# The prologue of a pooling and sparse-attention decoder step: keys' rows loaded ahead of the input, running means taken behind the pooling product, pooling groups in falling width

## The reference, cut to what matters

```
def _pool_mix(ext, pos0):              # ext: 15 earlier normed rows, then the new ones
    c = cumsum(ext, axis=1)
    for g, w in enumerate((2, 4, 8, 16)):
        s = c[..., 16:16+S, sl] - c[..., 16-w:16-w+S, sl]
        cnt = minimum(w, pos + 1)
        outs.append(s / cnt - xf[:, 15:, sl])

hn = _rmsnorm(h, norms_l[0])
ext = concatenate([buf, hn], axis=1)
mix = einsum('bsgc,gcd->bsgd', _pool_mix(ext, pos0), w_pool_l).reshape(B, S, D_MODEL) * scale_l
h = h + _rmsnorm(mix, norms_l[1])
```

## Time and profile before

| | |
|---|---|
| median of 3 runs | 2551.07 us (2548.14 to 2552.21) |
| profiled execution | 2551.54 us, of which the traced span is 2550.0 us |
| PE, PE weight loads | 2499.5 us (98%), 2462.4 us (97%) |
| DVE, ACT, POOL | 1195.7 us (47%), 924.1 us (36%), 268.3 us (11%) |
| DMA | 400.66 MB, mean 157 GB/s |
| first product that the result needs, pooling product, feed-forward group | start at 15.06, 50.21 and 114.01 us |

### The profile page before, as it was taken

How to read it: one execution, slowest core, us unless ns; L and a number is a source line. 1 busy time by engine, 2 the same in 40 slices (tenths; PEclk the granted TensorE clock), 3 DMA queues, 4 the chain that set the end, 5 groups by cost and what they waited for, 6 DMA issues and landing times.

```text
span 2550.0 us, 44217 instructions
## 1 busy us (share of the span) xinstructions
PE 2499.5 (98%) x17440; PEld 2462.4 (97%) x17440; DVE 1195.7 (47%) x1354; ACT 924.1 (36%) x1157; POOL 268.3 (11%) x316
## 2 busy tenths in 40 slices
PE   7999999999999999999999999999999999999997
PEld 7899999999999999999997799999999999999997
DVE  7564444444444444643535733744444444444444
ACT  5554233323332333632325633633233233323332
POOL 0420000000000001300002311400000000000012
PEclk9999999999999999999999999999999999999999
DMA  6444444444444444455445464344444444444443
GB/s 248 167 143 150 150 164 148 143 154 164 148 156 156 148 149 153 144 161 177 159 167 194 166 187 161 116 148 153 159 148 148 153 159 149 151 160 153 150 149 131
DMA packets 89738, 400.66 MB, mean 157 GB/s; under 512 B 13788, under 2 KB 24940, under 8 KB 60114
## 3 DMA queue, kind: packets, MB, share of 16 engines
q1 hardware_dynamic: 78066, 377.82, 43.7%
q0 software_dynamic: 6160, 12.60, 1.5%
q10 hardware_dynamic: 5456, 9.52, 1.1%
HBM read 392.16 MB, written 19.02 MB: 161 GB/s over the span
## 4 chain that ended last, share of the span: by engine, by line
PE 89%; DVE 5%; ACT 3%; issue 1%; POOL 1%; DMA 1%; SPq 0%; ACTq 0%; DVEq 0%
PE ps L1455 28%; PE ps L1456 28%; PE ps L1457 28%; PE ps L1556 2%; ACT w_hi L524 1%; DVE w_lo L863 1%; ACT y L631 0%; ACT x_hi L549 0%; DMA rowsK<-cmp_data_dram 0%; PE ps L1582 0%; POOL sc L1420 0%; DVE x_lo L881 0%; ACT sq L557 0%; DVE ps L905 0%; DMA rowsV<-cmp_data_dram 0%
## 5 line engine op out<-in xcount | busy, mean ns | idle before, releaser
L1455 PE MATMUL ps<-x_hi,w_hi 128*128 128x320 f32 x3536 | 1095.0, 310 | 6.7 <-DVE sg L1084 2.5
L1457 PE MATMUL ps<-x_hi,w_lo 128*128 128x320 f32 x3536 | 1093.1, 309 | 0.0
L1456 PE MATMUL ps<-x_lo,w_hi 128*128 128x320 f32 x3536 | 1093.1, 309 | 0.0
L863 DVE TENSOR_TENSOR w_lo<-w_raw,w_hi 128x2048 fp32r<-128x2048 f32 (+1 forms) x362 | 744.4, 2056 | 646.7 <-ACT w_hi L524 646.7
L524 ACT CAST w_hi<-w_raw 128x2048 fp32r<-128x2048 f32 (+1 forms) x362 | 619.0, 1710 | 506.1 <-PE ps L1457 479.6
L1455 PEld LDWEIGHTS ps<-x_hi,w_hi 128*128 128x128 f32 x3536 | 664.2, 188 | 9.1 <-DVE sg L1084 3.0
L1456 PEld LDWEIGHTS ps<-x_lo,w_hi 128*128 128x128 f32 x3536 | 664.2, 188 | 0.4 <-issue 0.2
L1457 PEld LDWEIGHTS ps<-x_hi,w_lo 128*128 128x128 f32 x3536 | 664.1, 188 | 0.0
L1457 PE MATMUL ps<-hid_hi,w_lo 128*128 128x320 f32 x1408 | 435.1, 309 | 0.0
L1455 PE MATMUL ps<-hid_hi,w_hi 128*128 128x320 f32 x1408 | 435.1, 309 | 0.0
L1456 PE MATMUL ps<-hid_lo,w_hi 128*128 128x320 f32 x1408 | 435.1, 309 | 0.0
(11 more groups left out here) (266 smaller groups left out, 1459.7 us busy)
## 6 DMA issues: line engine op xcount, KB each, us to landing
w_raw<-w_in_dram SPq DMA_DIRECT2D x176, 1024.0 KB, 4.9
w_raw<-w_out_dram SPq DMA_DIRECT2D x128, 704.0 KB, 4.1
w_raw<-w_kv_dram SPq DMA_DIRECT2D x24, 1024.0 KB, 6.8
w_raw<-w_q_dram SPq DMA_DIRECT2D x17, 1024.0 KB, 4.9
w_raw<-w_o_dram SPq DMA_DIRECT2D x15, 1024.0 KB, 5.2
win_out_dram<-win_kv_dram POOLq DMA_DIRECT2D x8, 992.0 KB, 5.4
rowsK<-cmp_data_dram SPq DMA_DIRECT2D x16, 256.0 KB, 9.0
pastK<-slc_k_dram SPq DMA_DIRECT2D x16, 256.0 KB, 3.5
```

The costliest lines, as they stand in the source:

```text
L863: V.tensor_tensor(w_lo[:, slot, 0:width], src, w_hi[:, slot, 0:width].bitcast(F32), ALU.subtract).then_inc(lo_made, 1)
L1455: M(out, wh, xh[:, k, :], start=(k == 0), stop=False)
L1456: M(out, wh, xl[:, k, :], start=False, stop=False)
L1457: last = M(out, wl, xh[:, k, :], start=False, stop=(k == kt - 1))
```

## The change

It touches the prologue alone; all products and outputs stay.

1. SP issues the keys' weights and the first eight keys' rows ahead of the input's four parts (the second half of `w1K` behind the fourth rows' transfer).
2. PE issues 16 warming products at once instead of 6 after the squares. The first 64 keys' products are done in halves of four pages each (`keys`), and the sum of squares lies between the fourth and the fifth product of the last sixteen. (Before, the second sixteen took all eight pages together.)
3. The pooling groups run in the order 3, 2, 1, 0 (`ORDER`), widths 16, 8, 4, 2.
4. DVE takes the running means of the samples alone ahead of the product (`sample_means`). The prompt goes into the product as it is, and its running means, less itself, are taken of the product's tiles in `y` (`prompt_means`), group by group, behind the splits of the panels. ACT's `square_y` waits for them (`pooled`).
5. ACT's list: `mix_high(1)` now stands behind `hi_split(1)` and `pool_tile(0)`; `save_states(2)` and `save_states(1)` ahead of `hi_split(0)`; all 16 tiles of `y` are copied by ACT; the four value rows that ACT issues lie between `pool_tile(8)` and `pool_tile(11)`, and all squares of `y` behind those.
6. The values' products are parted otherwise around the sums (24 and 4 ahead of them instead of 20 and 4).

```diff
-    w_rawX = at("w_rawX", "X", [P, PW], off=KT // 2 * NT * 4)
+    w_rawX = at("w_rawX", "X", [P, PW], off=0)
+    ORDER = tuple(reversed(range(NG)))
...
         sp.dma_start(pgs[:, :], pages[:, :]).then_inc(pages_in, 16)
-        for i in range(4):
-            sp.dma_start(h[:, i * GC:(i + 1) * GC, :], x[:, i * GC:(i + 1) * GC, :]).then_inc(x_in[i], 16)
         sp.dma_start(w1K[:, 0:CS, :], cmp_w1[0, :, 0:CS, :]).then_inc(w1K_in[0], 16)
         sp.wait_ge(pages_in, 16)
         for p in range(half):
+            if p == half // 2:
+                sp.dma_start(w1K[:, CS:CB, :], cmp_w1[0, :, CS:CB, :]).then_inc(w1K_in[1], 16)
             sp.dma_start(rowsK[0][:, p, :, :], cmp_data[0, page(p)]).then_inc(cmpK_in[p // (half // 2)], 16)
-        sp.dma_start(w1K[:, CS:CB, :], cmp_w1[0, :, CS:CB, :]).then_inc(w1K_in[1], 16)
+        for i in range(4):
+            sp.dma_start(h[:, i * GC:(i + 1) * GC, :], x[:, i * GC:(i + 1) * GC, :]).then_inc(x_in[i], 16)
...
ACT
-            if q == 1:
+            if q == 3:
                 act.dma_start(stS[:, :, :, :], st[:, :, :, :]).then_inc(st_in, 16)
+        def square_y(t):
+            act.wait_ge(pooled, t // GC + 1)
+            act.wait_ge(bank_read[t % 2], t // 2 + 1)
+            if t >= 2:
+                act.wait_ge(acc_made, t)
+            nc.scalar.square(sq[:, t % 2, :], y[:, feature(t), :]).then_inc(sq_made, 1)
...
         mix_high(0)
         act.wait_ge(st_set, 2)
         save_states(1)
+        save_states(2)
         hi_split(0, 0, src=w_rawX[:, :])
-        mix_high(1)
         save_states(3)
-        save_states(2)
         hi_split(1, 0, src=w_rawX[:, :])
         pool_tile(0)
+        mix_high(1)
+        for t in range(1, GC):
+            pool_tile(t)
         act.wait_ge(lo_made, 2)
         mix_high(2)
+        pool_tile(GC)
         hi_split(2, 0)
+        pool_tile(GC + 1)
+        mix_high(3)
+        pool_tile(GC + 2)
+        pool_tile(GC + 3)
         hi_split(3, 0)
...
+        for t in range(2 * GC, 3 * GC):
+            pool_tile(t)
+            past_values(2 * (t - 2 * GC) + 1)
+        for n in range(GC):
+            pool_tile(3 * GC + n)
+            square_y(n)
+        for t in range(GC, KT):
+            square_y(t)
...
DVE
+        def sample_means(n):
+            g = ORDER[n]
+            w = 2 ** (g + 1)
+            src, bufs = ext_s[:, g * GC:(g + 1) * GC, :, :], (winA, winB)
...
+            for m in range(g + 1):
+                d, dst = 2 ** m, bufs[m % 2][:, :, :].rearrange("p c (b j) -> p c b j", b=DB)
+                lo = BUF - (w - 2 * d)
+                link(V.tensor_tensor(dst[:, :, :, lo:EXT_B], src[:, :, :, lo:EXT_B], src[:, :, :, lo - d:EXT_B - d], ALU.add))
...
+        def prompt_means(n, between=lambda m: None):
+            g = ORDER[n]
+            w = 2 ** (g + 1)
+            x_ = y[:, g * GC:(g + 1) * GC, 0:SEQ]
+            bufs, lo = (postA, postB), BUF
+            if n:
+                dve.wait_ge(pooled, n)
+            for b_ in range(2):
+                dve.wait_ge(bank_read[b_], (n + 1) * GC // 2)
+            V.tensor_copy(postA[:, :, lo:lo + 1], x_[:, :, 0:1])
+            link(V.tensor_tensor(postA[:, :, lo + 1:lo + SEQ], x_[:, :, 1:SEQ], x_[:, :, 0:SEQ - 1], ALU.add))
+            between(0)
+            for m in range(1, g + 1):
+                d, src, dst = 2 ** m, bufs[1 - m % 2], bufs[m % 2]
+                link(V.tensor_tensor(dst[:, :, lo:lo + SEQ], src[:, :, lo:lo + SEQ], src[:, :, lo - d:lo + SEQ - d], ALU.add))
+                between(m)
+            total = bufs[g % 2][:, :, lo:lo + SEQ]
+            first = total[:, :, 0:w - 1]
+            link(V.scalar_tensor_tensor(out=first, in0=first, scalar=float(w), in1=rep(inv[:, g, 0:w - 1], GC),
+                                        op0=ALU.mult, op1=ALU.mult))
+            V.scalar_tensor_tensor(out=x_, in0=total, scalar=1.0 / w, in1=x_, op0=ALU.mult, op1=ALU.subtract).then_inc(pooled, 1)
...
         inputs(0)
-        window_sums(0)
+        sample_means(0)
         inputs(1)
-        window_sums(1)
+        inputs(2)
+        mix_low(0)
         inputs(3)
-        mix_low(0)
-        inputs(2)
         dve.wait_ge(cmp_half, 1)
         lo_split(0, 0, src=w_rawX[:, :])
-        window_sums(2)
+        sample_means(1)
         mix_low(1)
-        bias_rows(0, 4)
         lo_split(1, 0, src=w_rawX[:, :])
-        window_sums(3, between)
-        lo_split(3, 0)
+        sample_means(2)
+        mix_low(2)
+        sample_means(3)
+        lo_split(2, 0)
         mix_low(3)
+        prompt_means(0, split_between)        # lo_split(3) behind its first step
+        for n in range(1, NG):
+            prompt_means(n)
...
PE
-        pe.wait_ge(sqx_made, 4)
-        stay_warm(6)
+        stay_warm(16)
...
+        keys(0, 0, CS)
+        pe.wait_ge(w1K_in[1], 16)
+        keys(0, CS, CB)
+        pe.wait_ge(cmpK_in[1], 16 * (NP_ALL // 4))
+        keys(1, 0, CS)
+        pe.wait_ge(pos_in, 16)
+        pos_bias(4, 0, w1K)
+        keys(1, CS, CS + 4)
         pe.wait_ge(x_sum, 1)
         M(ps[:, STAT, 0:NT], ones[:, :], acc[:, :], start=True, stop=True).then_inc(stat_made, 1)
...
+        keys(1, CS + 4, CB).then_inc(cmp_half, 1)
```

More of the change, by code:

```diff
@@ L421, in _ @@
         sp.wait_ge(lo_made, 1)
-        sp.dma_start(w_rawX[:, :], w_pool[1]).then_inc(raw_in[1], 16)
+        sp.dma_start(w_rawX[:, :], w_pool[ORDER[1]]).then_inc(raw_in[1], 16)
         sp.wait_ge(cmp_sum, 1)
-        panel(2, 0, w_pool[2], PW)
-        panel(3, 0, w_pool[3], PW)
+        panel(2, 0, w_pool[ORDER[2]], PW)
+        panel(3, 0, w_pool[ORDER[3]], PW)
         sp.wait_ge(mix_made, NG)
@@ L647, in _, with gained @@
         sqrt_table()
[L648 to L653, removed]
+        def gained(n):
+            for k in range(GC):
+                i = ORDER[n] * GC + k
+                dst = hg_front[:, (n - 1) * GC + k, :] if n else hg_back[:, k, :]
+                A(dst, h[:, i, :], ACT.Copy, scale=gn[:, 0, i:i + 1]).then_inc(hgx_made, 1)
         def histories(lo, hi):
@@ L674, in save_states, with mix_high @@
+        def save_states(n):
+            c = slice(ORDER[n] * GC, (ORDER[n] + 1) * GC)
+            act.wait_ge(ext_made, n + 1)
             nc.scalar.copy(stP[:, c, :], ext[:, c, SEQ:EXT_P])
             nc.scalar.copy(stS[:, c, :, :], ext_s[:, c, :, DS:EXT_B]).then_inc(ext_saved, 1)
[L677 to L679 removed]
+        def mix_high(n):
+            act.wait_ge(mix_made, n + 1)
+            for dst, src in zip(by_tokens(x_hi, ORDER[n]), by_positions(ext, ORDER[n])):
@@ L680, in mix_high, with feature @@
                 last = nc.scalar.copy(dst, src)
             last.then_inc(mixhi_made, 1)
-        def pool_tile(n):
-            act.wait_ge(tile_made, n + 1)
-            A(y[:, n, :], ps[:, n % 2, 0:NT], ACT.Copy, scale=gn[:, G_POOL, n:n + 1]).then_inc(bank_read[n % 2], 1)
[L687 to L690, removed]
-            nc.scalar.square(sq[:, i % 2, :], y[:, i, :]).then_inc(sq_made, 1)
+        def feature(t):
+            return ORDER[t // GC] * GC + t % GC
@@ L996, in window_sums @@
                 src = dst
-                between(n)
-            (total, total_s), (x_, x_s) = by_positions(src, g), by_positions(ext, g)
-            first = total[:, :, 0:w - 1]
-            V.scalar_tensor_tensor(out=first, in0=first, scalar=float(w), in1=rep(inv[:, g, 0:w - 1], GC),
-                                   op0=ALU.mult, op1=ALU.mult)
-            full = rep(inv[:, g, CS - 1:CS].broadcast_to([P, DB * DS]), GC).rearrange("p c (b j) -> p c b j", b=DB)
-            link(V.tensor_tensor(total_s, total_s, full, ALU.mult))
@@ L1004, in window_sums @@
-            dve.wait_ge(ext_saved, (1, 2, 4, 4)[g])
-            V.scalar_tensor_tensor(out=x_, in0=total, scalar=1.0 / w, in1=x_, op0=ALU.mult, op1=ALU.subtract)
-            V.tensor_tensor(x_s, total_s, x_s, ALU.subtract).then_inc(mix_made, 1)
+            total, x_ = src[:, :, :, BUF:EXT_B], ext_s[:, g * GC:(g + 1) * GC, :, BUF:EXT_B]
+            full = rep(inv[:, g, CS - 1:CS].broadcast_to([P, DB * DS]), GC).rearrange("p c (b j) -> p c b j", b=DB)
+            link(V.tensor_tensor(total, total, full, ALU.mult))
@@ L1594, in _ @@
         turn_bias(4, 0)
-        for g in range(NG):
-            pe.wait_ge(lo_made, g + 1)
-            pe.wait_ge(mix_ready, g + 1)
+        for s in range(NG):
+            g = ORDER[s]
+            pe.wait_ge(lo_made, s + 1)
+            pe.wait_ge(mix_ready, s + 1)
             for n in range(GC):
-                t = g * GC + n
+                t = s * GC + n
                 if t >= 2:
```

140 lines of the change are left out of this document (59 added, 81 removed).

## The result

The changed kernel is slower: 2562.07 us (median of 5, 2559.78 to 2563.11) against 2551.07, a ratio of 1.0042 with a 95% interval of 1.0032 to 1.0053, that is 11.0 us or 0.4%. One execution of a later kernel (g_all), at 3935.8 us, belongs to a slow state and is left out of all comparisons. The profiled execution took 2559.78 us with a span of 2558.1; against the profiled 2551.54 of before that is 8.2 us.

What follows compares the result with a forecast made beforehand. PE was taken to bound the kernel, nine tenths of the span. G = 60.5 (second low part) + 61.1 (from there) + 1.0 (clock) = 122.6 against 114.0, +8.6: 2559.7, rounded down to 2559 us; 8-in-10 range 2549 to 2564.

Steps and rivals of the forecast that it cites:

- G: Start of PE's first feed-forward group, on which all later waits hang: 114.0 us before, forecast at 122.6.
- Part 1: PE's prologue: keys' products start at 10.5 instead of 18.42, PE ready for the pooling product at 43.7, 6.5 us earlier.
- Parts 2 and 3: Input loads and DVE's list: last input at 21.9 instead of 10.75, first low part at 44.4 instead of 38.3.
- Part 4: Second panel: lands at 53.1, ACT's order stops PE at the third tile until 55.2, second low part at 60.5.
- Rival C: Second panel lands fast, squares' sum late all the same: G at 119.3, +5.3 us, 2556.4; chance 0.15.
- Part 5: Second low part to G, 61.1 us: POOL's additions and DVE's means stretch each other, PE stands about 5.5 us.
- Rival B: POOL's additions of squares are hidden and stop nothing: G at 116.1, +2.1 us, 2553; chance 0.2.
- Part 6: PE's slow clock after the stops at the third tile and the sum: costs 1.0 us, bounds 0 and 3.4.
- Rival E: PE's head start holds, second panel early and additions hidden: G at 108.8, 2545.9 us; chance 0.05.

Runs made afterwards that it cites:

- g_all: Changed kernel with own buffer for second panel, second mixed group's high part before tile copies, 40 values' products before squares' sum, first-half keys' products before input's sum: 2546.25 us.
- i_warm_stops: Changed kernel with 12 useless warming products on PE ahead of the bias turn and 20 ahead of the sum of squares: 2559.07 us.
- d_refill: Changed kernel with the values' products parted otherwise, 40 instead of 24 ahead of the sum of squares and 16 instead of 28 behind the rows' factor: 2551.42 us.
- c_small_adds: Changed kernel with POOL's fifteen additions of squares taking one column instead of 320, the rest of the sum left out: 2551.05 us.
- a_list: Changed kernel with ACT's second mixed group's high part and first two tile copies moved ahead of the second panel's high part: 2560.28 us.
- b_panel: Changed kernel with the second pooling panel loaded into the space of its own low part, so that SP issues it earlier: 2557.47 us.
- j_three: Same as g_all but with the input's sum again between the fourth and fifth of the last sixteen keys' products: 2546.55 us.

## Why the prediction was right, step by step

| step | predicted | measured |
|---|---|---|
| first keys' product | 10.5 | 10.03 |
| last square of the input | 21.9 | 22.86 |
| first low part made | 44.4 | 44.67 |
| pooling product starts | 44.4 | 46.07 |
| second panel there | 53.1 | 51.71 |
| stop behind the second tile | 7.3 | 4.25 |
| second low part made (L) | 60.5 | 59.07 |
| squares' sum ready | L + 40.5 | 101.2, L + 42.1 |
| stops at bias and sum | 5.5 | 2.41 + 3.95 |
| slow clock behind bias and sum | 1.0 | 2.7 (22.59 less 19.90, i_warm_stops) |
| G | 122.6 | 123.81 |

*Part 1, the earlier start.* Right as far as it goes; the page list was there sooner (rows out at 3.22). PE reaches the pooling product at 46.07, 2.4 us later than the 43.7 of the sum. The wait for the input's sum is 3.21 and not 1.4, the input being 1 us later. The 64 products took 16.6 and not 15.3, as 24 of their records, right behind that wait, took 4.47 where they took 2.84 in d_refill: a slow clock that the prediction left out. (At the full clock all of them take 15.0, by d_refill, and not 13.6.) It cost nothing: where PE was ready at 44.5 and 44.7 (d_refill, c_small_adds), the third tile started at 54.0 and 54.2 all the same.

*Parts 2 and 3, the later input and DVE's list.* Right: `lo_made` 1 within 0.3 us of the sum made by steps.

*Part 4, the second panel.* Right in mechanism, and a_list and b_panel show it. The load took 7.0 and not 8.8, with the store of the states issued 0.5 us ahead of it, so L came 1.4 sooner. Rival C had the right direction for it but not the size. The products behind the stop ran at the low level (0.27 us apart instead of 0.15, up to 58.8) and put group 1 at 59.82, 0.75 behind L: here the clock was not hidden as I had said.

*Part 5, the squares.* Right that the additions and the means would stretch each other and that PE would stand for it, and this is the largest term: c_small_adds takes the whole 11.0 us away. Rival B falls with it. The make-up was another one. I had twelve additions beside the means, each costing DVE 0.5 to 0.68. The size was right (0.55), but only eight such waits fitted in, since each addition stood for a pass of DVE as well and took 1.86; so the means lost 4.4 us and not 6 to 8, and ended at 94.17, L + 35.1. In exchange six additions were left behind them, where I had the last four squares, and the sum was ready 7.0 us later: 1.6 later than forecast in all. That small instructions pay the wait for the long one behind them I had left out.

*Part 6, the clock.* The mis-sized term: I took 1.0, the traces have 2.7. I had thought of the clock as something lost while PE comes back from a stop; the low level lasted from about 96.4 to 106.6, so it covered all work in the 5 us behind the sum. That two stops lie close together may not be needed for it: behind the single stop of 4.25 us at the third tile the low level lasted for 4.7 us of work too.

*Rival E, the head start holds.* Its condition named the second panel, and the panel was late; but j_three shows that the head start itself can be had when the panel and the squares are out of the way, 2.6 us of it.

*The size.* G was forecast at 122.6 and came at 123.81, and that is in part luck: L came 1.4 too soon, the squares' sum 1.6 too late after it, and the stretch from the sum to G took 22.59 instead of 21.6 (0.7 less for the products, 1.7 more for the clock). The forecast of +8.6 for the profiled execution stands against 8.2 there. G moved by 9.8 and the span by 8.1, so from G to the end this trace is 1.7 us shorter. That alone does not speak against the claim that all behind G only moves: over the twelve traces that distance is 2434.1 to 2438.1 us (before 2436.0, changed 2434.3, g_all 2438.1) and doesn't follow what was done in the prologue. A part of it is a wait of PE for DVE's tile `sg` between 1530 and 1730, of 1.1 us in before and d_refill and 2.7 in changed, b_panel and g_all; the rest is open. That the medians differ by 11.0 fits another number: the changed kernel's profiled execution is the fastest of its five. In the nine traces with keys first the input's sum reached PE at 27.09 to 30.02, and in this one at 27.16, nearly the earliest. That this makes up the 3 us is argued and not shown. So the median came 3 us above the 2559 that was forecast, and those 3 us are in no term of the sum.

By the rule of the Trainium skill, "SBUF — State Buffer", section "Who interferes with whom" (two SBUF inputs on DVE and a reading GpSimd instruction exclude each other for the whole instruction), each addition should have cost DVE its full 1.02, an estimate that takes the measured 1.02 for the whole instruction. The additions of one column in c_small_adds agree with the exclusion: 0.79 and 0.93 beside DVE, 0.19 alone. The size doesn't: each of the eight waits cost DVE about 0.55 and not 1.02. Why no more than that part of an addition shuts DVE out, no run here shows.

## What to carry to other kernels

Work that is moved behind a product isn't free because its engine has room there: ask which other engine works in that place, whether the two shut each other out, and who waits for the later of them. While DVE's means and POOL's additions ran together, an addition took 1.86 instead of 1.02 us and DVE's list 15.2 instead of 10.8, and the cheapest mend was not to part them but to give PE work to do in the meantime (10.6 us for moving sixteen products). Mends of different stops add up (4.6 for the panel's buffer and 10.6 for the refill are 15.2; j_three, which has both, gained 15.5); two mends of the same stops, the small additions (11.0) and the refill (10.6), can't both be had. An early start is worth what the next shared buffer lets through: here PE was at the pooling product 4.1 us sooner, and group 1 still started 2.5 us later, at a panel that could not be asked for before the first had been used up.

## What the hardware showed that I had not expected

- The time at which the input's sum is there varies once 4 MB of other loads go ahead of it: 27.09 to 30.02 in nine traces with the keys first, 14.94 to 15.06 in three with the input first.
- The granted clock stayed at 0.50 for some 10 us (about 96.4 to 106.6) over and behind two stops of 2.4 and 4.0 us, though PE worked in the second half of that time. Where 7.2 us of useless products were put into the stops, it never fell.
- A GpSimd addition of one column took 0.19 us alone and 0.79 to 0.93 beside DVE; a DVE copy of four elements 0.17 alone and 0.72 beside GpSimd. The long DVE pass right behind such a copy kept its 1.22: the wait was paid once, by the instruction in front.
